# A two-layer decoder step on one core: modulation rows computed in another place, the first norm's shift and scale held as columns, masks loaded on change, a shorter triangular inverse

## The reference, cut to what matters

```python
mod = jax.nn.silu(c) @ w_ada + b_ada                 # 9 rows: 1 prompt, 8 samples; 6 * 1024 columns
sh1, sc1, g1, sh2, sc2, g2 = jnp.split(mod, 6, axis=-1)
h = _rmsnorm(x, norm1_g) * (1 + sc1) + sh1           # first norm
proj = h @ w_in                                      # conv, query, z and "misc" columns
a_mat = strict_lower(beta * kk * decay) + eye        # per head; solved by a triangular inverse
x = x + g1 * (mix @ w_out)
h2 = _rmsnorm(x, norm2_g) * (1 + sc2) + sh2          # second norm
x = x + g2 * _peer(h2, ...)                          # 128 experts for each token, gathered rows of 1024
```

## Time and profile before

| | us |
|---|---|
| three runs | 4344.15, 4345.22, 4350.73 (median 4345.22) |
| the profiled execution | 4338.44, of which the span from first to last instruction 4336.6 |
| busy in the span | TensorE 3660.1, VectorE 2698.8, GpSimd 2348.3, ScalarE 1034.7 |
| first gather of an expert row issued | 476.17 |

### The profile page before, as it was taken

One profiled execution on the slowest core, in us unless ns is written; L12 is line 12 of the kernel. 1 busy time (PEld: TensorE's weight loads), 2 busy tenths in 40 slices (PEclk: granted clock), 3 DMA queues, 4 the chain that ended last, 5 costly groups with the idle time before them and its releaser, 6 DMA issues.

```text
span 4336.6 us, 45555 instructions
## 1 busy us (share of the span) xinstructions
PE 3660.1 (84%) x15180; PEld 2168.1 (50%) x15180; DVE 2698.8 (62%) x6307; ACT 1034.7 (24%) x2478; POOL 2348.3 (54%) x2218
## 2 busy tenths in 40 slices
PE   7778789888888888879888888888888888899766
PEld 1546356544644555656456444644564455456522
DVE  1234674876776586538667666776587657664575
ACT  0111322232132222112321322132213121312122
POOL 0000475477467547434764577467647764674455
PEclk9888899999999999889999999999999998998989
DMA  7626799999999999699999999999999999997988
GB/s 272 256 100 224 285 389 406 376 375 399 395 363 384 379 382 347 250 322 377 378 356 384 348 394 391 414 375 405 393 414 381 387 389 366 377 364 298 331 327 341
DMA packets 362538, 1527.72 MB, mean 352 GB/s; under 512 B 44952, under 2 KB 46872, under 8 KB 340512
## 3 DMA queue, kind: packets, MB, share of 16 engines
q0 software_dynamic: 316480, 1151.48, 69.7%
q1 hardware_dynamic: 39632, 316.42, 18.6%
q10 hardware_dynamic: 6192, 56.91, 3.5%
HBM read 1505.45 MB, written 21.22 MB: 352 GB/s over the span
## 4 chain that ended last, share of the span: by engine, by line
PE 48%; DVE 21%; DMA 14%; issue 7%; POOL 6%; ACT 4%; SPq 0%; DVEq 0%; POOLq 0%; ACTq 0%
PE ACC L1387 20%; DVE ubuf L1133 6%; PE B L1191 6%; DMA vbuf<-in_peer_v,idxs 5%; PE B L1367 4%; DMA ubuf<-in_peer_u,idxs 4%; PE ACC L1159 3%; DMA W<-in_w_big 3%; PE B L1354 3%; POOL ubuf L526 3%; POOL vbuf L535 3%; PE B L1198 2%; PE B L1222 1%; PE B L1169 1%; DVE qkvT L854 1%
## 5 line engine op out<-in xcount | busy, mean ns | idle before, releaser
L1387 PE MATMUL ACC<-vbuf,diag 128*128 128x512 f32 x4352 | 2092.6, 629 | 381.4 <-ACT diag L725 221.2
L526 POOL DMA_INDIRECT ubuf<-in_peer_u,idxs x1088 | 1181.8, 1086 | 1396.8 <-issue 735.1
L1387 PEld LDWEIGHTS ACC<-vbuf,diag 128*128 128x128 f32 x4352 | 838.6, 202 | 1431.4 <-issue 1017.1
L535 POOL DMA_INDIRECT vbuf<-in_peer_v,idxs x1088 | 1150.2, 1057 | 566.0 <-issue 325.8
L1133 DVE CUSTOM_DVE_ANT_0 ubuf<-ubuf,h2p 128x1024 f32<-128x1024 f32 x960 | 1141.8, 1221 | 183.1 <-DMA ubuf<-in_peer_u,idxs 182.6
L725 ACT ACTIVATE diag<-ident,a 128x128 f32<-128x128 f32 x1024 | 355.4, 395 | 966.2 <-DVE a L1092 959.7
L733 ACT ACTIVATE a<-a 128x2 f32<-128x2 f32 x544 | 110.5, 203 | 864.8 <-DVE a L1133 864.3
L1367 PEld LDWEIGHTS B<-hT,W 128*128 128x128 f32 x2560 | 296.4, 195 | 31.3 <-issue 29.6
L1191 PEld LDWEIGHTS B<-hT,W 128*128 128x128 f32 x2560 | 297.3, 196 | 25.9 <-issue 14.9
L1367 PE MATMUL B<-hT,W 128*128 128x128 f32 x2560 | 297.9, 278 | 10.7 <-DMA W<-in_w_big 10.1
L1191 PE MATMUL B<-hT,W 128*128 128x128 f32 x2560 | 298.5, 279 | 9.6 <-DMA W<-in_w_big 8.3
(11 more groups left out here) (252 smaller groups left out, 3331.4 us busy)
## 6 DMA issues: line engine op xcount, KB each, us to landing
W<-in_w_big SPq DMA_DIRECT2D x110, 2048.0 KB, 10.8
ubuf<-in_w_ada ACTq DMA_DIRECT2D x16, 2048.0 KB, 8.4
ubuf<-in_peer_u,idxs POOLq DMA_INDIRECT x1088, 6.9
vbuf<-in_peer_v,idxs POOLq DMA_INDIRECT x1088, 7.0
vbuf<-in_w_ada ACTq DMA_DIRECT2D x8, 2048.0 KB, 8.7
W<-dram_mod SPq DMA_DIRECT2D x10, 1536.0 KB
W<-in_w_misc SPq DMA_DIRECT2D x10, 1056.0 KB, 8.2
W<-dram_mod SPq DMA_DIRECT2D x10, 1024.0 KB
```

The lines of the kernel that those rows point to most:

```text
L526: g.indirect_dma_start(out=ubuf[:, i % R, e % G, :], out_offset=None, in_=ins["peer_u"], in_offset=off).then_inc(u_in[e % SLOTS_UV], 16)
L535: g.indirect_dma_start(out=vbuf[:, v // G % R, v % G, :], out_offset=None, in_=ins["peer_v"], in_offset=off).then_inc(v_in[v % SLOTS_UV], 16)
L1387: last = T.matmul(ACC[c][:], diag[:, i % R, j, :], vbuf[:, i % R, j, 512 * c:512 * c + 512], start=k + j == 0, stop=k == end - 1 and j == ...
```

## The change

- The four chunks that hold the shift and scale of the first norm run ahead of unit 0 (`FIRST`), the other twenty inside it: `MOD_SEAMS` gets one chunk at each of `half0` to `half6` and one at `conv0` of the joint seams.
- For these four chunks of either layer TensorE transposes the finished row in four pieces of 9x128 (after VectorE's addition), and VectorE copies the result to `modT`, one column to a vector of 128 channels.
- The first norm only multiplies by the reciprocal root (one operation on 128x1024). For prompt tiles shift and scale are applied when ScalarE takes `hT` out of PSUM: eight operations of 128x128 with a bias and a scale per partition, where there were two copies of 128x512. For the unit of the samples VectorE does it in two operations for each half.
- `mod_a` is gone from `CHUNKS`; `W` alternates without regard to the unit (`SIDE`), and the next unit's first two blocks can follow wq2 and wq3.
- SyncE waits for the stores of `mod` only ahead of the first `mod_b`.
- `masks` is loaded whole for the first tile and for the unit of the samples, 128 columns of it for tile 1, and not at all for tiles 2 and 3.
- Level 0 of the inverse: `XT` is the identity minus `BT`, and `X` the identity minus four transposes of `BT`. The last level leaves `X` alone. The two copies of the identity are gone.

The core of the diff:

```diff
-CHUNKS = ["mod_a", "conv0", "conv1", "conv2", "swq", "z", "misc", "state", "cache",
+CHUNKS = ["conv0", "conv1", "conv2", "swq", "z", "misc", "state", "cache",
-MOD_SEAMS = dict(swq=1, z=1, misc=1, qkv=1, decay=1, kk=1, state=1, scores=1, softmax=1, pv=1, conv2=1, hswq=1)
+FIRST = 4
+MOD_SEAMS = dict(swq=1, z=1, misc=1, qkv=1, decay=1, kk=1, **{f"half{i}": 1 for i in range(LEVELS)},
+                 state=1, scores=1, softmax=1, pv=1, conv0=1, conv2=1, hswq=1)
...
-            for _ in rows(0):
-                pass
-            spare = rows(1)
+            spare = rows()
+            for _ in range(FIRST):
+                next(spare)
...
+                if tile == 0 or batch:
+                    sp.dma_start(masks[:], ins["masks"][tile]).then_inc(masks_in, 16)
+                elif tile == 1:
+                    sp.dma_start(masks[:, 2 * P:3 * P], ins["masks"][tile, :, 2 * P:3 * P]).then_inc(masks_in, 16)
...
+                    if c == "mod_b" and tile == 0:
+                        for even_odd in mod_out:
+                            sp.wait_ge(even_odd, 16 * 5 if u == 0 else 8 * MB * L)
...
-                    A.copy(hT[:, 4 * i:4 * i + 4, :], four(B[i])).then_inc(s["hT_sb"], 1)
+                        for k in range(4 * i, 4 * i + 4):
+                            last = A.activation(hT[:, k, :], four(B[i])[:, k - 4 * i, :], ACT.Identity,
+                                                bias=modT[:, layer, k, 0:1], scale=modT[:, layer, KC + k, 0:1])
...
+                    if j < FIRST:
+                        dve.wait_ge(modT_ps, FIRST * l + j + 1)
+                        V.tensor_copy(modT[:, l, 4 * j:4 * j + 4, :], ACC[n % 2][:, 0:36].rearrange("p (k c) -> p k c", c=9)).then_inc(modT_sb, 1)
...
-                last = V.scalar_tensor_tensor(out, src, rs, gain, ALU.mult, ALU.mult)
-                if shift is not None:
-                    link(last)
-                    last = V.tensor_tensor(out, out, shift, ALU.add)
+                if gain is None:
+                    return V.tensor_scalar(out, src, rs, None, ALU.mult)
...
+                    if j < FIRST:
+                        pe.wait_ge(mod_sb, n + 1)
+                        for q in range(4):
+                            last = T.transpose(ACC[n % 2][:, 9 * q:9 * q + 9], modrow[n % 4][:, P * q:P * q + P], ident[0:9, 0:9])
...
+                    if i == 0:
+                        turn(lambda j: BT[:, j, :], B[2:3], "xu_ps", none)
+                        yield "half0"
+                        yield "level0"
+                        continue
...
-                        T.matmul(B[2][:, P * hh:P * hh + P], XT[:, hh, :], U1[:, hh, :], start=True, stop=True)
+                        if i + 1 < LEVELS:
+                            T.matmul(B[2][:, P * hh:P * hh + P], XT[:, hh, :], U1[:, hh, :], start=True, stop=True)
```

More of the change, by code:

```diff
@@ L259, in program @@
         def program(head, body, tail, step, rows):
-            for _ in rows(0):
-                pass
-            spare = rows(1)
-            for seam in head(0):
-                if seam == "conv0":
-                    next(spare)
+            spare = rows()
+            for _ in range(FIRST):
+                next(spare)
+            for seam in head(0):
+                pass
             for u in range(DUES):
@@ L375, in keep_cache @@
                                      kvtok[lo:lo + 4, 1, n * P:(n + 1) * P]).then_inc(cache_out, 16)
-            freed = dict(mod_a=("h_normed", 1), conv0=("conv_ps", 1), conv1=("conv_ps", 2),
-                         conv2=("conv_ps", 3), swq=("swq_ps", 1), z=("z_ps", 1),
-                         misc=("misc_ps", 1), wo0=("wo_ps", 1), wo1=("wo_ps", 2),
-                         mod_b=("h2_sb", 1), wq0=("wq_ps", 1), wq1=("wq_ps", 2),
-                         wq2=("wq_ps", 3), cache=("pv_ps", 1), before0=("wq_ps", -1), before1=("wq_ps", 0))
+            freed = dict(conv0=("conv_ps", 1), conv1=("conv_ps", 2), conv2=("conv_ps", 3), swq=("swq_ps", 1), z=("z_ps", 1),
+                         misc=("misc_ps", 1), cache=("pv_ps", 1), wo0=("wo_ps", 1), wo1=("wo_ps", 2), mod_b=("h2_sb", 1),
+                         wq0=("wq_ps", 1), wq1=("wq_ps", 2), wq2=("wq_ps", 3), wq3=("wq_ps", 4))
+            last = [None, None]
             for u in range(DUES):
@@ L823, in norm @@
                 link(V.reciprocal(rs, ss))
-                last = V.scalar_tensor_tensor(out, src, rs, gain, ALU.mult, ALU.mult)
-                if shift is not None:
-                    link(last)
-                    last = V.tensor_tensor(out, out, shift, ALU.add)
-                return last
+                if gain is None:
+                    return V.tensor_scalar(out, src, rs, None, ALU.mult)
+                link(V.scalar_tensor_tensor(out, src, rs, gain, ALU.mult, ALU.mult))
+                return V.tensor_tensor(out, out, shift, ALU.add)
             def head(u):
                 wait = waiter(dve, u)
+                layer, tile, batch = place(u)
                 wait("x_in", 16)
-                dve.wait_ge(w_in["mod_a"], 16 * (u + 1))
-                norm(wait, 1, x[:], h[:], A1, sh1).then_inc(s["h_normed"], 1)
+                norm(wait, 1, x[:], h[:], None, None).then_inc(s["h_normed"], 1)
+                if batch:
+                    for i in range(2):
+                        wait("hT_ps", i + 1)
+                        k = slice(4 * i, 4 * i + 4)
+                        shift, gain = (modT[:, layer, n + 4 * i:n + 4 * i + 4, 1:9] for n in (0, KC))
+                        out = hT[:, k, :].rearrange("p k (b t) -> p k b t", b=NB)
+                        full = [P, 4, NB, SLOTS]
+                        link(V.tensor_tensor(out, B[i][:].rearrange("p (k b t) -> p k b t", k=4, b=NB),
+                                             gain.unsqueeze(3).to_broadcast(full), ALU.mult))
+                        V.tensor_tensor(out, out, shift.unsqueeze(3).to_broadcast(full), ALU.add).then_inc(s["hT_sb"], 1)
                 yield from HEAD
@@ L840, in body @@
                 h2, cw = h2s[u], cws[:, layer, :, :]
+                g1, sh2, A2 = (wslot(u, "mod_b")[:, i * D:(i + 1) * D] for i in range(3))
+                SS = old_state(u) if batch else None
                 wait("misc_sb", 1)
@@ L918, in body @@
                 V.tensor_tensor(BT[:], AT, again(level[0], H), ALU.mult).then_inc(s["level_b"], 1)
+                wait("level_b", 1)
+                V.tensor_tensor(XT, again(ident[:], H), BT[:], ALU.subtract)
                 for i in range(LEVELS):
@@ L1190, in head @@
                         for k in range(KC):
-                            last = T.matmul(B[2 + i][:, P * j:P * j + P], blocks(c)[:, j, k, :], hT[:, k, :],
+                            last = T.matmul(B[2 + i][:, P * j:P * j + P], blocks(u, c)[:, j, k, :], hT[:, k, :],
                                             start=(k == 0), stop=(k == KC - 1))
@@ L1197, in head @@
                 for k in range(KC):
-                    last = T.matmul(B[0][:], hT[:, k, :], cols("z")[:, k, :], start=(k == 0), stop=(k == KC - 1))
+                    last = T.matmul(B[0][:], hT[:, k, :], cols(u, "z")[:, k, :], start=(k == 0), stop=(k == KC - 1))
                 last.then_inc(s["z_ps"], 1)
@@ L1353, in body @@
                     for k in range(KC):
-                        last = T.matmul(B[i][:], hT[:, k, :], cols(f"wo{i}")[:, k, :], start=(k == 0), stop=(k == KC - 1))
+                        last = T.matmul(B[i][:], hT[:, k, :], cols(u, f"wo{i}")[:, k, :], start=(k == 0), stop=(k == KC - 1))
                     last.then_inc(s["wo_ps"], 1)
```

180 lines of the change are left out of this document (92 added, 88 removed).

## The result

The kernel after takes **4274.3 us** (median of four runs, 4272.9 to 4282.4) beside 4344.7 us for the kernel before: a ratio of 0.9839 with a 95% interval of 0.9823 to 0.9855, that is 70 us less, between 63 and 77. A second set of runs, on another chip, gave 4270.0 beside 4343.8, ratio 0.9833 (0.9816 to 0.9850). The forecast was 4298, 47 us less; its range held the time, its sum fell some 23 us short.

What follows compares the result with a forecast made beforehand. Up to about 475 us a plain sequence with nothing full bounds the kernel; afterwards DMA engines and TensorE are near full and alternate in ending last. Start -22 and full part -25 make -47: 4345.2 to 4298 us, range 4268 to 4327.

Steps and rivals of the forecast that it cites:

- The start, -22: Before the first gather: -65 to conv0 and first projection, +1 late load, +36 levels, +6 joint seams; between -36 and -6.
- The 6 us for new traffic: Ahead of unit 0, x, masks and two W blocks delay the chunk loads: 6 us taken, between nothing and 13.4.
- Bytes, -9 of 0 to 30: Units 2 to 9, mod_a and mask loads dropped, 11.9 MB: 9 us less taken, bounds 0 and 30.
- The inverse, -9: Full part, nine units: 3.7 us of TensorE less per unit, 33 at most; 1 a unit taken.
- full part: The span after gathers begin, DMA engines and TensorE near full: -25 us from bytes, norm and inverse, between 0 and -60.
- The norm, -7 of 0 to 15: Six prompt heads: the shift's 1.23 us goes from TensorE's wait, 7 us; a shorter multiplication, 0 to 8 more, taken as 0.
- The samples' two heads: Two units' heads: VectorE waits for transposes and makes four operations, saves two; a microsecond or two each, taken as nothing.
- DMA last everywhere: Rival, full part: DMA engines end last, all 30 us of bytes and half the inverse count: -75, 4270; chance 0.15.
- Full part nothing: Rival: TensorE and DMA engines take turns, one uses up what the other saves: -22, 4323; chance 0.10.
- both nothing: Rival: neither start nor full part gives anything: 4345, no change; chance 0.08.
- Start nothing: Rival: low clock in levels (16) and late first chunk (7) cancel the start; -25 from the rest, 4320; chance 0.10.
- Slower: Rival: in unit 0's levels chunk loads come one seam late, seven uncovered, 59 us: +12, 4357; chance 0.05.

Runs made afterwards that it cites:

- second dose: Kernel after with whole masks in every unit and a further 2 MB copy at the head of units 1 to 9, 23.1 MB more: 4300.1 us, ratio 0.9889.
- second trace: Profiled execution of the second set of runs of the unchanged kernel after: span 4262.0 us; that set's median 4270.0 us, ratio 0.9833.
- longer norm: Kernel after with the norm's last multiplication made three times instead of once, 1.5 us more in each unit's head: 4295.6 us, ratio 0.9879.
- five traces: After, after again, twelve chunks ahead, chunks at the ends of levels, W behind the third chunk: first gathered rows to end, 3809 to 3823 us.

## Why the prediction was right, and where it was too small

The sign, the places and the order of the dates were right. The sum was too small, with no one term far off: the bytes and the inverse were sized somewhat low, and the norm's term was met partly by luck.

**The start, -22.** Measured -23 in the first pair of traces and -28 in the second. Its steps held one by one: the norm at 53.8 (54 foretold), conv0 at 60.5 (61), the end of the first projection at 106.4 (107), the levels in 88.1 us (87.6) at a clock of 0.98 (166 to 254 us). The 6 us for new traffic were near the lower bound, and rightly: the third load took 10 us longer than in before, but holding `W` back gave only 2 to 4 us of the path, since TensorE had the first two chunks to work on meanwhile. The rest of the 6 is matmuls slower than the 7.0 us a chunk that was counted, 9.26 us for the first and 8.74 for the third. The Trainium skill, "DMA: Bandwidth & Descriptors", section "Queues, rings and completion order", has each DMA engine take turns between the queues that have work. The stretched load agrees in kind; the delay near the upper bound of 13.4 that the prediction worked out from it does not show on the path.

**Bytes, -9 of 0 to 30.** Right in kind: neither 0 nor all. Two doses give 1.0 us per MB, so the 11.9 MB after the first gather are about 12 us, by a copy that also writes; the rest of the second dose's trace, 25 us longer than the mean, says 13.

**The inverse, -9.** About 11 in the full part, by the edit alone and undone.

**The norm, -7 of 0 to 15.** Two of its choices were wrong and nearly cancel. The multiplication that lost an operand was taken to stay as long as it was; it lost 0.53 us, so the six prompt heads after the first gather have 1.79 us less norm each and not 1.23. The Trainium skill, "VectorE: DVE Perf Modes", section "Mode 2×_2P — use both read ports for one tensor", has a float32 operation with one tensor in SBUF run two elements at a time; 0.75 against 1.28 agrees nearly. From the start of the norm to conv0 these six heads take 117.2 us together instead of 127.0 (118.8 in the second trace). The samples' two heads were taken as nothing; by the same two dates they became 3.2 us longer together (1.6 in the second trace), with VectorE's four operations in between. That leaves 6.6 and 6.5 us, 8 at the price of the longer norm, where 19 us came of 15.7 (ten heads at 1.57). So the 7 stands, in part by luck. In the heads of units 0 and 1 ScalarE's eight operations, 2.91 us, give back most of the 1.79: 0.3 to 0.4 is left of it.

**The sum.** The start gave 23 to 28 where 22 stood. The rest became 38 us shorter by the mean of five traces (3855.4 to 3817), where 25 stood; the bytes with 12 to 13, the inverse with 11 and the norm with 7 to 8 make 30 to 32 of it. What is left to the 70 and 73 measured is mostly that the profiled execution of before lies 6 us under its median. So of the 23 us that the forecast fell short, up to 6 lie in the start, 5 to 6 in bytes and inverse, and about 6 in the profiled execution; for some 6 more in the rest the runs name no cause, and they are no more than one trace can scatter.

**The rivals.** *DMA last everywhere* gave the right time by the wrong mechanism: its bytes cost some 40% of what it asks. *Full part nothing* falls with the rest, 38 us shorter, and with the second dose of bytes; *both nothing* falls with the time. *Start nothing* falls with the dates. *Slower*, by uncovered chunk loads in the levels, did not happen: TensorE waits for no load there.

**Not settled:** whether the price of the head's norm is TensorE's wait or VectorE's delay of the choice of experts, as 1.5 us more of norm in each unit cost some 13 to 21 us even where TensorE hardly waits for it; and the 14 us between the two profiled executions and the medians, which lie within what runs of one kernel differ by (before was seen from 4329 to 4366).

## What to carry to other kernels

A wait of an engine that is 85% busy, and that comes at the same place in every unit with nothing else in its queue to do, counted nearly in full here. Price it by all of its operations and all of its units, and set against it what the same change adds behind it, as in the samples' heads. Then ask whether its producer has an idle stretch earlier in its own order, and how long that stretch is in each unit: moving the norm there gave about half as much again as the whole change. A byte in a stretch where the DMA engines show a share of 1.00 need not cost its own time: two doses of extra bytes measure its price. A load's time is compared with that of the same load in the other kernel, with the same loads ahead of it. A time that meets a rival's number says nothing of the rival's mechanism until a run doubles its cause.

## What the runs showed of the hardware that was not expected

- The float32 multiplication of 128x1024 by a scalar per partition took 0.75 us; with a second tensor as operand it took 1.28.
- The third of three chunk loads issued together landed after 26.7 and 25.1 us with `x`, masks and two blocks of `W` beside it, after 19.7 with `W` held back, and after 16.6 in the kernel before. TensorE's path lost 2 to 4 us by the early `W`.
- The granted clock over the levels was 0.69 in before (232 to 284 us) and 0.65 with twelve chunks ahead (224 to 277), both without chunks in them; 0.98 and 0.96 in the two traces of after, with a chunk in the middle of each level (166 to 254, 163 to 252); and 0.90 with a chunk at the end of each (168 to 254). A value between 0.50 and 1.00 is part of a stretch at 1.2 instead of 2.4 GHz. These are single traces, and no run shows what made the difference.
- One MB more on SyncE's queue cost about 1.0 us at the heads of the units, where the DMA share was 0.94 in before: some 40% of the 2.5 us that it takes at 396 GB/s.
